# Weaving the next head's projections between the tiles of a two-map attention, and fuller shapes for left-over rows

## The reference

```python
# two-map ("diff") attention, 8 heads, each with two score maps of width 64
s = jnp.einsum('bqhmd,bkhmd->bhmqk', qb, k).astype(jnp.float32) * scale
dist = jnp.where((qp[:, None] < N_META) | k_meta[None, :], 0.0, dist)
s = s - slopes[None, :, None, None, None] * dist
p = jax.nn.softmax(s, axis=-1)
w = p[:, :, 0] - lam * p[:, :, 1]
return jnp.einsum('bhqk,bkhe->bqhe', w.astype(v.dtype), v)

# expert choice: each of 16 experts takes its 130 best tokens (cap = 2 * 1040 // 16)
top_aff, top_idx = lax.top_k(jnp.swapaxes(aff, 1, 2), cap)
xs = jax.vmap(lambda ub, ib: ub[ib])(u, top_idx)
hid = jax.nn.silu(xs @ w_gate) * (xs @ w_up)
y = (hid @ w_down) * top_aff[..., None]          # added back at top_idx
```

## Time and profile before

| | us |
|---|---|
| median of 3 runs | 3807.99 (3806.25 to 3811.59) |
| profiled execution, its own time | 3809.24 |
| its span, first to last instruction | 3807.1 |
| PE busy (matmul) | 3518.0, 92% |
| PE weight loads | 3032.4, 80% |
| DVE, ACT, POOL busy | 1419.5, 991.5, 781.9 |
| mean granted TensorE clock | 0.96 of full speed |

### The profile page before, as it was taken

How to read it: one execution, slowest core, us unless ns; L and a number is a source line. 1 busy time by engine, 2 the same in 40 slices (tenths; PEclk the granted TensorE clock), 3 DMA queues, 4 the chain that set the end, 5 groups by cost and what they waited for, 6 DMA issues and landing times.

```text
span 3807.1 us, 54098 instructions
## 1 busy us (share of the span) xinstructions
PE 3518.0 (92%) x20966; PEld 3032.4 (80%) x20966; DVE 1419.5 (37%) x2330; ACT 991.5 (26%) x1723; POOL 781.9 (21%) x515
## 2 busy tenths in 40 slices
PE   8999988999999989999999999899999999699996
PEld 6666766888887868888888899777777999489996
DVE  3454343000004545555555520645555133511212
ACT  3232241000001224444444410244144211311112
POOL 3112203232322332111111132100100122012121
PEclk9999989999999999999999999999999999799998
DMA  3001112111112120000000011100000121468786
GB/s 144 23 22 33 33 56 78 50 44 50 44 49 89 50 84 18 17 19 25 17 17 17 11 42 58 68 1 11 23 1 11 55 90 56 157 232 274 267 271 220
DMA packets 69590, 268.89 MB, mean 71 GB/s; under 512 B 9249, under 2 KB 9889, under 8 KB 68753
## 3 DMA queue, kind: packets, MB, share of 16 engines
q1 hardware_dynamic: 62304, 228.81, 17.3%
q0 software_dynamic: 5632, 17.05, 2.0%
q10 hardware_dynamic: 1584, 22.07, 1.4%
HBM read 229.55 MB, written 38.34 MB: 70 GB/s over the span
## 4 chain that ended last, share of the span: by engine, by line
PE 54%; DVE 4%; issue 2%; ACT 1%; DMA 0%; POOL 0%; ACTq 0%; DVEq 0%; POOLq 0%; SPq 0%
PE PS L511 23%; PE PS L499 6%; PE PS L2207 6%; PE PS L2096 4%; PE PS L2215 3%; PE PS L1950 3%; PE PS L1909 3%; PE PS L2075 3%; PE PS L2097 1%; PE PS L1951 1%; DVE EA L1586 1%; PE PS L2019 1%; PE PS L2062 1%; PE PS L2024 0%; PE PS L1922 0%
## 5 line engine op out<-in xcount | busy, mean ns | idle before, releaser
L511 PE MATMUL PS<-u_hi,w_hi 128*128 128x512 f32 (+1 forms) x2464 | 661.4, 363 | 39.9 <-DVE u_lo L465 11.5
L511 PE MATMUL PS<-u_lo,w_hi 128*128 128x512 f32 (+1 forms) x2464 | 653.5, 360 | 0.0
L511 PE MATMUL PS<-u_hi,w_lo 128*128 128x512 f32 (+1 forms) x2464 | 648.7, 358 | 0.0
L533 POOL CAST w_hi<-ring 128x1024 fp32r<-128x1024 f32 x174 | 183.0, 1052 | 1805.0 <-PE PS L511 1608.9
L511 PEld LDWEIGHTS PS<-u_hi,w_hi 128*128 128x128 f32 x2464 | 439.0, 190 | 114.5 <-issue 51.5
L511 PEld LDWEIGHTS PS<-u_hi,w_lo 128*128 128x128 f32 x2464 | 441.6, 189 | 57.1
L511 PEld LDWEIGHTS PS<-u_lo,w_hi 128*128 128x128 f32 x2464 | 443.0, 189 | 54.1
L535 POOL TENSOR_TENSOR w_lo<-ring,w_hi 128x1024 fp32r<-128x1024 f32 x174 | 419.6, 2411 | 14.0
L904 DVE TENSOR_TENSOR hid<-sq,PS 128x1024 f32 x22 | 26.9, 1221 | 457.9 <-PE PS L511 457.9
L1349 ACT ACTIVATE EA<-EA,small_sb 128x1040 f32<-128x1040 f32 x144 | 166.4, 1155 | 90.2 <-DVE small_sb L1586 90.1
L1586 DVE CUSTOM_DVE_ANT_0 EA<-PS,biasH,low_a 128x1024 f32<-128x1024 f32 x128 | 163.4, 1281 | 25.8 <-PE PS L1909 25.1
(11 more groups left out here) (332 smaller groups left out, 5274.3 us busy)
## 6 DMA issues: line engine op xcount, KB each, us to landing
ring<-in_stream SPq DMA_DIRECT2D x174, 512.0 KB, 3.5
w_gate_sb<-in_w_gate SPq DMA_DIRECT2D x64, 512.0 KB, 3.9
w_up_sb<-in_w_up SPq DMA_DIRECT2D x64, 512.0 KB, 7.1
w_down_sb<-in_w_down SPq DMA_DIRECT2D x64, 512.0 KB
x_keep<-xT ACTq DMA_DIRECT2D x2, 4176.0 KB, 13.0
xT<-x_keep ACTq DMA_DIRECT2D x1, 4176.0 KB, 12.9
x2T<-x_keep ACTq DMA_DIRECT2D x1, 4176.0 KB, 14.0
x_keep<-x2T SPq DMA_DIRECT2D x1, 4176.0 KB, 13.8
```

What stands on the lines that cost most here:

```text
L511: last = mm(bank(to_bank, width), w[j][:, c, :], src[:, c, b * width:(b + 1) * width], start=(c == 0 and k == 0), stop=(c == KD - 1 and k ...
L533: pool.tensor_copy(w_hi[j][:, :, :], w_raw[j][:, :, :]).then_inc(S["w_rounded"], 1)
```

## The change

1. **Weaving.** Stage A is written as one pipeline over all heads. k, q and v of head h + 1 are projected during head h in nine pieces (`UNITS`), one per tile: one third of 348 columns of one of the three tiles, 24 matmuls into the one bank 4, cut in two halves of 12 that stand before and behind the transposes. Head 0's projections stand alone, with its first scores inside v; the last head has none to carry; the first tile of the merge stage takes its last transposes and values in.
2. Around it: both maps of a tile are scored together one tile ahead; the second map has one buffer (EA2) instead of two; keys are rounded straight from PSUM by ACT, and their remainder formed by DVE from PSUM, per third, in two sets of buffers; the meta scores of the next head come in two parts (5 and 4 tiles) behind tiles 5 and 8; the meta column of the transposes goes first, into bank 7; DVE does reduce, reduce, combine of one tile in a row. POOL halves the bias behind the three splits of a head. The weight tiles come in the order k, q, v.
3. **Padded meta pieces.** The 16-row piece of the values has 128 rows, zeros below (Va_meta and Vb with zeroed rest, PTa and PTb too), in both attentions.
4. **Left-over tokens in 16 pieces.** The 2 left-over tokens of an expert are gathered as 16 rows of 128 numbers (8 chunks x 2), so one transpose takes them in, and one takes their results back; their rows go out as 16 pieces. The indices are formed once after the top-k, by replicating and scaling (8 x index + chunk).

```diff
+UNITS = [("k", 0), ("k", 1), ("k", 2), ("q", 0), ("q", 1), ("v", 0), ("v", 1), ("q", 2), ("v", 2)]
+WEAVE = 4
+EARLY = 5
+PIECES = REST * KD
...
@@ POOL
+                split(pool, A0 + 2, 0, A0 // 2 + 2, A0)
+                with pool.Fori(0, (HEADS - 2) // 2) as i:
+                    for j in range(2):
+                        for x in range(3):
+                            n = A0 + 6 * i + 3 * j + 3 + x
+                            split(pool, n, (3 * j + 3 + x) % 2, A0 // 2 + 3 * i + (3 * j + 3 + x) // 2 + 1, n - 2)
+                        halve_bias(2 * i + j + 1)
...
@@ ACT, one head
                     for t in range(NT + 1):
+                        if before:
+                            result(*before)
...
+                        if after:
+                            exp(after[0], (after[1] + after[2]) % 2, after[2], 0)
+                        if before:
+                            square(*before)
+                        take_pt_meta(h, par, t, first and t < 2)
+                        if after:
+                            exp(after[0], (after[1] + after[2]) % 2, after[2], 1)
+                        take_pt(h, par, t)
+                        if not last:
+                            kind, c = UNITS[t]
+                            unit_done(h + 1, kind, c)
+                            take_unit(h + 1, 1 - odd, kind, c, WEAVE)
...
@@ DVE
+                def attend(h, par, t, fresh=False):
+                    scores(h, par, t, 0, fresh)
+                    scores(h, par, t, 1, fresh)
+                    combine(h, par, t, fresh)
...
+                    dve.wait_ge(S["ob_q"], z0 + GROUP + 1)
+                    for rest in (Vb, *PTb):
+                        dve.memset(rest[:, NT, :], 0.0).then_inc(S["bb_z"], 1)
...
+                    dve.wait_ge(S["ex_yt"], e * 4 + 3)
+                    dve.tensor_copy(y_rest[:, :, :], yT[:, :, P:CAP]).then_inc(S["ex_yt"], 1)
...
@@ TensorE
+                def unit(h, odd, kind, c, half):
...
+                    for d in range(half * HALF, (half + 1) * HALF):
+                        for k, (w, src) in enumerate(((w_hi, u2_hi), (w_hi, u2_lo), (w_lo, u2_hi))):
+                            last = mm(bank(WEAVE, CH), w[slot][:, d, :], src[:, d, columns_of(c)], start=(d == 0 and k == 0), stop=(d == KD - 1 and k == 2))
...
+                def values(h, odd, t, done):
...
+                    mm(bank(7, P, 0, m), PTa[par][:, NT, 0:m], Va_meta[odd][:, :], start=False, stop=True).then_inc(S["aa_o"], 1)
...
+                def head(h, odd, first=False):
+
+                    for t in range(NT + 1):
+                        if t < NT:
+                            scores(h, odd, t + 1, first)
+                        else:
+                            scores(h + 1, 1 - odd, 0)
...
+                        kind, c = UNITS[t]
+                        unit(h + 1, 1 - odd, kind, c, 0)
+                        turn_probs(h, (odd + t) % 2, t, first)
+                        unit(h + 1, 1 - odd, kind, c, 1)
                         if t >= 1:
+                            values(h, odd, t - 1, 18 * h + 2 * t + 1)
...
+                head(0, 0, first=True)
+                with pe.Fori(0, (HEADS - 2) // 2) as i:
+                    head(2 * i + 1, 1)
+                    head(2 * i + 2, 0)
...
-                        mm(bank(7, m), Vb[0:META, NT, :], PTb[t % 2][0:META, NT, 0:m], start=False, stop=True).then_inc(S["bb_o"], 1)
+                        mm(bank(7, m), Vb[:, NT, :], PTb[t % 2][:, NT, 0:m], start=False, stop=True).then_inc(S["bb_o"], 1)
...
                     for c in range(KD):
-                        turn(bank(2 + c // 3, P, (c % 3) * CAP), xs[0][:, c * P:(c + 1) * P])
-                        last = turn(bank(2 + c // 3, REST, (c % 3) * CAP + P), xs[1][:, c * P:(c + 1) * P], REST)
+                        last = turn(bank(2 + c // 3, P, (c % 3) * P), xs[0][:, c * P:(c + 1) * P])
+                        if c == KD - 1:
+                            last = turn(bank(4, PIECES, 2 * P), xs[1][:, :], PIECES)
...
+                    pe.wait_ge(S["ex_yt"], e * 4 + 4)
+                    turn(bank(7, P, 0, PIECES), y_rest.rearrange("p c n -> p (c n)")).then_inc(S["ex_r"], 1)
                     for n in range(2):
-                        pe.wait_ge(S["ex_yt"], e * 3 + 2 + n)
                         for c in range(4):
-                            turn(bank(5 + n, P, c * P), yT[:, 4 * n + c, 0:P])
-                            last = turn(bank((7, 0)[n], P, c * P, REST), yT[:, 4 * n + c, P:CAP])
+                            last = turn(bank(5 + n, P, c * P), yT[:, 4 * n + c, 0:P])
```

More of the change, by code:

```diff
@@ L1165, in pairs @@
                                 also(n - first)
-                pairs(MG0 + 2, B0 + 2)
+                pairs(A0 + 2, B0 + 2)
                 sp.wait_ge(S["w_used"], tile_done(B0 - 1))
@@ new lines, in result, with square @@
+                def result(h, t):
+                    m = P if t < NT else META
+                    act.wait_ge(S["aa_o"], 9 * h + t + 1)
+                    seen(act)
+                    act.activation(o_tok[0:m, t, bass.ds(h * P, P)], bank(7, P, 0, m), ACT.Copy,
+                                   scale=small[0:m, 20 + t % 3:21 + t % 3]).then_inc(S["aa_y"], 1)
+                def square(h, t):
+                    m = P if t < NT else META
+                    act.wait_ge(S["aa_y"], 9 * h + t + 1 + CREDIT)
+                    act.activation(junk[0:m, :], o_tok[0:m, t, bass.ds(h * P, P)], ACT.Square,
+                                   accum_out=ss2[0:m, t, bass.ds(h, 1)]).then_inc(S["aa_ssq"], 1)
+                    act.wait_ge(S["aa_ssq"], 9 * h + t + 1)
@@ L1376, in sigmoid @@
+                with act.Fori(0, (HEADS - 2) // 2) as i:
+                    head(2 * i + 1, 1)
+                    head(2 * i + 2, 0)
+                head(HEADS - 1, 1, last=True)
+                for t in (NT - 1, NT):
+                    result(HEADS - 1, t)
+                    square(HEADS - 1, t)
                 def sigmoid(d, j, n, first):
@@ L1623, in _ @@
+                for c in range(3):
+                    lower_keys(0, 0, c, c)
+                for c in range(3):
+                    lower_queries(0, c)
+                meta_scores(0, True)
+                attend(0, 0, 0, True)
+                meta_scores(0, False)
+                head(0, 0, first=True)
+                with dve.Fori(0, (HEADS - 2) // 2) as i:
+                    head(2 * i + 1, 1)
+                    head(2 * i + 2, 0)
+                head(HEADS - 1, 1, last=True)
                 dve.wait_ge(S["as_sd"], 1)
@@ new lines, in _ @@
+                pe.wait_ge(S["aa_qs"], 3)
+                project_split(pe, 0, A0 + 2, (6, 7, 4), CH, u2_hi, u2_lo, start_first)
+                head(0, 0, first=True)
+                with pe.Fori(0, (HEADS - 2) // 2) as i:
+                    head(2 * i + 1, 1)
+                    head(2 * i + 2, 0)
+                h = HEADS - 1
+                for t in range(NT):
+                    scores(h, 1, t + 1)
+                    if t == 0:
+                        pe.wait_ge(S["aa_vf"], 3 * h + 3)
+                        pe.wait_ge(S["aa_pt"], 18 * h)
+                        turn(bank(6, P, 0, META), vTa[:, T1:T2]).then_inc(S["aa_v"], 1)
+                    turn_probs(h, (1 + t) % 2, t, False, False)
+                    if t >= 1:
+                        values(h, 1, t - 1, 18 * h + 2 * t + 1)
+                    else:
+                        values(h - 1, 0, NT, 18 * h + 1)
+                        pe.wait_ge(S["aa_pt"], 18 * h + 2)
+                        turn_values(h)
```

547 lines of the change are left out of this document (307 added, 240 removed).

## The result

The changed kernel takes 3677.99 us (median of 4 runs, 3672.89 to 3683.16), the kernel before beside it 3809.79 (3806.25 to 3816.46): ratio 0.9655, interval 0.9632 to 0.9678. The profiled execution took 3672.89 us with a span of 3671.1, that is 136.0 less than the span before.

A forecast was written before the change was run, and what follows sets the result against it. TensorE was taken to bound the kernel. Stage A -55.4, grouped-query stage -11.6 and experts -38.9 sum to -106 from 3809.2, forecast as a median of 3702 us, range 3684 to 3738.

The forecast's parts named there:

- "2.10 us" for half a piece: Stage A, woven heads: 12 projection matmuls in four groups, 0.58 + 3 x 0.48 + 0.08 = 2.10 us.
- "1.58 + 2 x 2.10 + 1.04 + 2.10 = 8.92 us": Stage A, one woven loop: scores, two half pieces, transposes, padded values; giving 83.2 us a head instead of 93.1.
- Start, last head and end: Stage A around the seven woven heads: head 0's q and v projections 28.7 us, last head 64, first merge tile 16.5.
- "7.2": Last head of stage A: loop of 7.2 us against 4.92 before, with a 2.4 us hole, before any clock effect.
- the 0.8 a loop set aside for the clock: Last head: loop taken as 8.0 us, between 7.2 without clock effect and 10.5 with all matmuls at half speed.
- "-0.185 for each of 64 tiles": Grouped-query stage: padding cuts a 16-row piece from 0.41 to 0.225 us; stage -11.6, ends 0 and -13.
- Experts: Gaps between experts: fewer transposes, DVE's copies leave 2.5 us of 5.00; -2.5 for each of 15 gaps, -38.9 in all.
- The padding's: Rival, both attentions: padding the meta pieces is worth nothing, 26 us less gain, 3728; chance 4%.
- the last head's clock: Rival, stage A: the last head falls to the lower clock throughout, +20 us, 3722; chance 8%.
- the transfers: Rival, experts: bound by transfers, DMA share 0.88 instead of 0.80; gaps shrinking by 1 us only, +22, 3724; chance 10%.
- the dearer piece: Rival, woven loops: 12 matmuls in a piece dearer than in a projection, weight load setting the pace, +45 us, 3747; 8%.
- a slower kernel: Rival, woven loops: TensorE waits for the combine in every loop and the clock halves, +186 us, about 3888; chance 2%.

## Why the prediction was right, and where it failed

- **In short:** the change does what the prediction said, for the reasons that it gave, but the time lies 6 us outside the range. Two terms of the sum were mis-sized, both towards too little gain: the loop of a woven head and the padded piece in the grouped-query stage.
- **Bound, direction and mechanism: right.** TensorE's row is the chain before and after. The woven loops have no hole, the pieces cost what their matmuls cost plus 0.1 us for the first, and what the weaving removes is the holes at the start of a head (57.8 us of waits before, 27.1 after). The low clock behind them, which the earlier trace rows show in the trace before, is no fixed part of it: with the same holes, six of these eight heads ran at 1.00 in another trace.
- **"2.10 us" for half a piece and "1.58 + 2 x 2.10 + 1.04 + 2.10 = 8.92 us": the step that failed in stage A.** The terms took a dearer first and a dearer last group for every change of kind of work, because that is how the rows around a projection look. In the loop the first matmul of a piece costs 0.27 or 0.24 instead of 0.16, and the last nothing more. With 1.61 for the scores, 2.01 + 1.98 for the pieces, 0.90 for the transposes instead of 1.04, and 2.10 for the values (as forecast) the loop is 8.60. A head is 80.0 instead of 83.2 us. Seven heads took 567.2 us and not 582.4, although two jumps back gave 9 us of the gain away, which no term had.
- **Start, last head and end: right.** 27.1 against 28.7, 64.9 against 64, 16.5 against 16.5. The hole behind the transposes is 2.34 against "2.4". The loop at the full clock is 7.30 against "7.2"; the 0.8 a loop set aside for the clock was 6.4 us in all, and 10 us at the lower level cost about 5. That the first tile, with the value transposes, is some 2 us longer had no term, so the match to 1 us is partly luck.
- **"-0.185 for each of 64 tiles": the step that failed in the grouped-query stage.** The row of the piece was read and its neighbours' were not. The piece costs 0.19 itself, and 0.16 in the work on both sides of it, whose weight loads it holds up: 0.34 to 0.35 a tile, -20.9 for the stage, beyond the end of -13 that I had given.
- **Experts: right.** 24.81 us a period against 24.8; the gate projection starts 0.1 us after DVE's last xsT (a wait too short for the profile to bracket); -39.5 with the indices, against -38.9.
- **Rivals.** The padding's was the weakest of all: alone it is worth 28 us, where the prediction itself said 26 and the rival 0. TensorE: Matmul & The Clock Gate of the Trainium skill (LDWEIGHTS) says that row count does not matter to a weight load. For the load by itself the trace agrees (0.29 and 0.30 us for two). Taken as a rule for the kernel's time, the runs with 16, 32 and 64 rows would have equalled the padded ones, and the measurement decides against that. TensorEngine Tiling (Array Packing) of the Trainium skill (Key Properties) says that a change of tiling mode drains the engine. If a change of row count is such a change, the trace agrees: the loads of the piece and behind it are no longer ahead. Of the last head's clock the lower level came for 10 of 65 us, not throughout; the transfers and the dearer piece did not come; a slower kernel was nowhere near, since the combine is done 4.1 us before its transposes' turn (1629.49 and 1633.55; 4.6 had been forecast).
- **The range** ended 6 us above the result. It was built around two terms that both erred towards too little gain, and its lower end lay 18 us below the sum. The two stages missed by 16 and 9, and block 1 added 4 by chance.

## What to carry to other kernels

A matmul with another row count in a chain of full ones is charged to three rows of the timeline: read the pitch from neighbour to neighbour, not that matmul's row alone, and pad it with zeros where there is room. See first whether another engine is about to bind: in the old order of stage A half of the padding's gain went into a wait for DVE. Before a difference between two traces is put down to an edit, compare a stage that neither edit touches. Don't add a switch cost for each change of kind of work before the timeline of just that pair of kinds shows it. A stage that is woven needs its old order where nothing is left to weave in, and a body long enough for weaving may be dearer to jump back to than to write out.

## What the hardware showed that was not expected

- A piece of 16, 32 or 64 rows costs the same, 0.41 or 0.42 us for two passes instead of 0.22 among 128-row work and 0.32 ahead of 64-row work. The 16 passes ahead of it take 0.10 more, and 128-row transposes behind it 0.06 more.
- A jump back over two heads' instructions stopped TensorE for 2.8 and 2.9 us, and the matmuls behind it stood 0.29 apart instead of 0.16 for some 3 us, at a granted clock of 0.50.
- The same instructions of one grouped-query group took 301.8 us at a granted clock of 0.98 and 316.0 at 0.93. The two places some 20 us apart in which runs of several of these kernels fall go with the run's mean granted clock (0.961 to 0.964 and 0.955 to 0.957); which stretch differs in them was not seen, as no run of a padded kernel at the lower mean was profiled. This stays open.
- The same holes of 1.95 us at the start of a head had the lower level of the clock at them or just behind them in all eight heads of the trace before, and in none of the heads from the second to the seventh in the trace of the left-over pieces alone. What decides this no run here shows.
- DVE's combine of 1040 columns took 3.25 us instead of 1.30 where POOL's subtraction of 2.34 us ran beside it; the slack hid it.
